# Cached keys of the samples' attention: turned by transposing DMAs on two-byte halves instead of by TensorE

## The chip, the cores and the metric

The kernel runs on one core of one Trainium2 chip. The metric is the device time of one execution in microseconds. The kernel before takes 1761.27 us (median of three runs, 1759.50 to 1762.44).

## The reference: what is computed

One layer of a decoder, for a prompt of 1024 tokens and for 8 samples with 4 new tokens each (1056 tokens in all, width 1024): a mixer (windowed attention beside a convolution), cross-attention into 256 memory tokens, and a gated feed-forward part with a short convolution. The part that the change touches is the attention of the samples in the mixer:

```python
def dilated_branch_sample(q, kc, vc, dil):
    # q: (Bd,T,H,Dh); kc,vc: (Bd, WB+T, H, Dh) = window buffer then new rows
    j = jnp.arange(KEYS_PER_BRANCH + 1)
    idx = wb + jnp.arange(T)[:, None] - dil * j[None, :]
    kg = kc[:, idxc]
    s = jnp.einsum("bthd,btjhd->bthj", q, kg) * (HEAD_DIM ** -0.5)
    ...
    o = jnp.einsum("bthj,btjhd->bthd", (p / den).astype(vc.dtype), vg)
```

It is done for the dilations 1, 4 and 16 over cached keys and values of 2048 rows of 512 numbers (8 heads of 64, float32) for each sample. Of the 2048 cached rows only 896 are ever read: the last 512, and of the older ones four rows in every sixteen (384). To score them, the head dimension must lie on the partitions, while the cache in HBM has a row per key: the keys have to be turned.

## The kernel before, in words

Everything stays in float32. The large products (input projections, output, cross-attention and feed-forward weights) run over weight units of 128 output columns: SyncE loads a unit (`weight`, line 460) into one of four ring slots (`raw`), ScalarE rounds it to a high part (line 621), VectorE makes the low part (line 1854), and TensorE does three products. The last input unit is `LAST_IN`; its end opens the attention stage.

The attention stage is one loop over steps `s`, written out by hand on each engine. A step is a pair of heads for 128 prompt queries: `STEPS` has 32 of them, 8 query tiles (`i`) times 4 pairs, and a step grows with `i`. Step `s` runs the scores of `s`, the transposes of the probabilities of `s - 2`, the product with V of `s - 3`. Between these pieces lie up to three slots a step, and slots carry the samples' work: 88 slots, 44 for each group of 4 samples (`first_slot`, `sample_slot`). The first 14 steps have three slots each, the later ones 2 or 3. In a group, slots 0 to 27 turn the key tiles (a sample has 7 tiles of 128 keys, `KTILES`), slots 1 to 28 score them, slots 29 to 34 do the softmax and turn the probabilities, slots 35, 37, 39 and 41 multiply by the values of one sample each, and slots 42 and 43 take the result out. Each engine has its own `sample(g, r)` for its share. All engines work in order, so a late key tile holds everything behind it.

The key path before: SyncE loads a window (`window`, line 472: 896 rows of one sample, keys or values, in four DMAs) into one of three buffers `cached`, in the order four key windows, four value windows, and so on (`ORDER_W`). In a key slot TensorE turns four 128 x 128 blocks of a tile into one PSUM bank (`key_turn`, line 1427, recorded under line 1237); ScalarE (line 801) or VectorE (line 2071) copies the bank to `KTS`, a third to two thirds of the tiles each (`on_scalar`); and in the next slot TensorE scores the tile (`key_scores`, line 1436, recorded under line 1240): four products for the four pairs of heads, each into its own 32 rows of a bank, against `QW`, which holds the samples' queries spread with zeros.

```python
        def key_turn(n):
            b, a = divmod(n, KTILES)
            w, c = window_of("k", b)
            take(4 + n % 2, "ktsa" if on_scalar(n) else "ktsd", n)
            pe.wait_ge(*at(f"cached{c}", (w, OLD // P - 1)))
            for k in range(AT):
                ins = turn(bank[4 + n % 2][:, k * P:(k + 1) * P], cached[c][:, a, k * P:(k + 1) * P])
            ins.then_inc(*mark("ktr", n))
```

SyncE's queue around it (lines 506 to 529): the weights up to the third output unit are issued before the last input product ends, then window 1 after it, window 2 after the convolution's tiles are free, the 19 output DMAs of V, of the convolution state and of the copied state (lines 512 to 519), then windows 3 to 15, each behind a wait for the window that its buffer held (`ktr` for keys, `spv` for values), then the fourth output weight. GpSimd does a few memsets (lines 597 to 608) and nothing else.

## Time and profile before

| | |
|---|---|
| median of 3 runs | 1761.27 us (1759.50 to 1762.44) |
| span of the profiled execution | 1761.8 us |
| attention stage | 335 to 545 us of the span |
| HBM read / written | 220.68 MB / 11.50 MB |
| mean granted clock of TensorE | 0.995 |

The page gives no time of its own for the profiled execution beside its span, from the first to the last instruction; the span is 0.5 us above the median of the runs. Line numbers are those of the kernel before. A float32 product is recorded as two instructions, a transpose as one: a row of "x8" products is four, a row of "x4" transposes is four. "128*32" before the shape is the size of the stationary part. A helper records many operations under one line: 1237 is every transpose of TensorE, 1240 every product, 458 every load of SyncE. "SPq" is SyncE issuing a DMA, and its time is that of the issue, not of the transfer. In a timeline the first column is the start in the span, the second how long the row lasts; the ends of products overlap the next row's start, so the pitch from start to start is what one takes.

### The profile page before, as it was taken

The page shows a single profiled execution, that of the slowest core. Times are in us where ns is not written, and L with a number is a line of the kernel's source. Part 1 is how long each engine was busy: PE and PEld are TensorE (multiplying, and loading weights), DVE is VectorE, ACT ScalarE, POOL GpSimd, SP SyncE. Part 2 cuts the span into 40 slices and gives each one's busy share as a digit, 9 for nine tenths or more (in the row PEclk, how much of TensorE's full clock was granted, in tenths as well). Part 3 has the DMA queues.
Part 4 walks back from the last instruction along what each step waited for, and adds up shares of the span by engine and source line. Part 5 has one row for each costly group of instructions (what it writes and reads, how often), then busy time and mean ns, then how long its engine had stood idle before and what let it go on. Part 6 is the DMA issues. An engine that isn't in the chain of part 4 may idle for free.

```text
span 1761.8 us, 30467 instructions
## 1 busy us (share of the span) xinstructions
PE 1712.2 (97%) x12158; PEld 1595.8 (91%) x12158; DVE 1127.0 (64%) x2077; ACT 876.3 (50%) x1645; POOL 2.2 (0%) x12
## 2 busy tenths in 40 slices
PE   7999999999999999999998999999999999999998
PEld 7999999756668999888778899999999999999998
DVE  5499998686675677345467667644576533676633
ACT  7322223655667676555455455534545533555433
POOL 0000000000000000000000000000000000000000
PEclk9999999999999999999999999999999999999999
DMA  8233221365315645443533334444445444444443
GB/s 247 64 119 114 84 86 37 132 225 192 127 43 154 185 144 156 149 131 108 164 120 96 118 114 140 133 136 138 133 143 155 139 140 139 132 144 147 144 136 100
DMA packets 349219, 233.74 MB, mean 133 GB/s; under 512 B 7979, under 2 KB 322465, under 8 KB 349071
## 3 DMA queue, kind: packets, MB, share of 16 engines
q1 hardware_dynamic: 344232, 222.96, 41.4%
q10 hardware_dynamic: 4847, 8.83, 1.4%
q8 instruction: 98, 1.61, 0.4%
q14 instruction: 42, 0.34, 0.1%
HBM read 220.68 MB, written 11.50 MB: 132 GB/s over the span
## 4 chain that ended last, share of the span: by engine, by line
PE 85%; DVE 7%; ACT 4%; issue 3%; SPq 1%; DMA 0%; ACTq 0%; DVEq 0%
PE bank L1240 79%; PE bank L1237 6%; ACT whi L621 1%; SPq L458 1%; DVE cv L1841 1%; DVE wlo L1854 1%; DMA raw<-in_w_mk_dram 0%; DVE Y L1841 0%; DVE Pp L1845 0%; DVE RSCF L1977 0%; DVE Pp L2130 0%; ACT wide L635 0%; DVE op_lo L1841 0%; DVE XT L2232 0%; DVE C L1981 0%
## 5 line engine op out<-in xcount | busy, mean ns | idle before, releaser
L1240 PE MATMUL bank<-op_hi,whi 128*128 128x352 f32 x1632 | 539.5, 331 | 4.9 <-DVE wlo L1854 2.6
L1854 DVE TENSOR_TENSOR wlo<-raw,whi 128x1024 fp32r<-128x1024 f32 (+1 forms) x312 | 373.8, 1200 | 246.0 <-ACT whi L621 245.7
L1240 PE MATMUL bank<-op_hi,wlo 128*128 128x352 f32 x1632 | 525.4, 322 | 0.0
L1240 PE MATMUL bank<-op_lo,whi 128*128 128x352 f32 x1632 | 524.5, 321 | 0.0
L621 ACT ACTIVATE whi<-raw 128x1024 fp32r<-128x1024 f32 (+1 forms) x312 | 325.1, 1043 | 287.7 <-PE bank L1240 94.5
L1240 PEld LDWEIGHTS bank<-op_hi,whi 128*128 128x128 f32 x1632 | 307.5, 188 | 14.6 <-issue 9.9
L1240 PEld LDWEIGHTS bank<-op_lo,whi 128*128 128x128 f32 x1632 | 308.4, 189 | 0.6
L1240 PEld LDWEIGHTS bank<-op_hi,wlo 128*128 128x128 f32 x1632 | 307.3, 188 | 0.0
L1240 PE MATMUL bank<-fhi,whi 128*128 128x352 f32 x528 | 171.2, 324 | 0.0
L1240 PE MATMUL bank<-fhi,wlo 128*128 128x352 f32 x528 | 170.7, 323 | 0.0
L1240 PE MATMUL bank<-h1hi,whi 128*128 128x352 f32 x480 | 158.0, 329 | 0.0
L1841 DVE SCALAR_TENSOR_TENSOR C<-U,cw,C 128x1024 f32<-128x1024 f32 x120 | 154.1, 1284 | 3.8
L1240 PE MATMUL bank<-h1hi,wlo 128*128 128x352 f32 x480 | 154.3, 321 | 0.0
L1240 PE MATMUL bank<-h1lo,whi 128*128 128x352 f32 x480 | 154.0, 321 | 0.0
L1240 PEld LDWEIGHTS bank<-fhi,wlo 128*128 128x128 f32 x528 | 99.8, 189 | 0.0
L1240 PEld LDWEIGHTS bank<-fhi,whi 128*128 128x128 f32 x528 | 99.4, 188 | 0.0
L1240 PEld LDWEIGHTS bank<-h1lo,whi 128*128 128x128 f32 x480 | 90.3, 188 | 0.6
L1240 PEld LDWEIGHTS bank<-h1hi,whi 128*128 128x128 f32 x480 | 90.1, 188 | 0.7
L1240 PEld LDWEIGHTS bank<-h1hi,wlo 128*128 128x128 f32 x480 | 90.1, 188 | 0.0
L1240 PE MATMUL bank<-flo_a,whi 128*128 128x352 f32 x264 | 84.9, 322 | 0.0
L1841 DVE SCALAR_TENSOR_TENSOR cv<-aext,fw,cv 128x352 f32<-128x352 f32 (+2 forms) x176 | 81.0, 491 | 3.9
L2205 DVE TENSOR_TENSOR Sy<-Sy,SQy 128x352 f32<-128x352 f32 x63 | 33.0, 524 | 70.6 <-ACT SQy L898 70.5
(287 smaller groups left out, 2299.7 us busy)
## 6 DMA issues: line engine op xcount, KB each, us to landing
raw<-in_w_up_dram SPq DMA_DIRECT2D x132, 512.0 KB, 3.7
raw<-in_w_down_dram SPq DMA_DIRECT2D x48, 512.0 KB, 3.7
raw<-in_w_out_dram SPq DMA_DIRECT2D x24, 512.0 KB, 3.8
raw<-in_w_xq_dram SPq DMA_DIRECT2D x24, 512.0 KB, 3.8
raw<-in_w_xo_dram SPq DMA_DIRECT2D x24, 512.0 KB, 3.8
raw<-in_w_in_dram SPq DMA_DIRECT2D x20, 512.0 KB, 3.8
raw<-in_w_down_dram SPq DMA_DIRECT2D x24, 384.0 KB, 3.3
cached<-in_cache_win_k_dram SPq DMA_DIRECT2D x8, 1024.0 KB, 5.9
```

The costliest lines, as they stand in the source:

```text
L458: sp.dma_start(dst, src).then_inc(*mark(name, key, 16))
L621: act.activation(whi[v % SLOTS][:, 0:nk, :], raw[v % SLOTS][:, 0:nk, :], ACT.Copy).then_inc(*mark("w_hi", v))
L1237: return pe.transpose(out, in_, ident[r:r + n, r:r + n])
L1240: return pe.matmul(out, lhsT, rhs, start=first, stop=last, skip_group_check=shared)
L1841: return dve.scalar_tensor_tensor(out=out, in0=in0, scalar=scalar, in1=in1, op0=op0, op1=op1)
L1854: dve.tensor_tensor(wlo[v % SLOTS][:, 0:nk, :], raw[v % SLOTS][:, 0:nk, :], whi[v % SLOTS][:, 0:nk, :].bitcast(F32), ALU.subtract).then_in ...
L2205: dve.tensor_tensor(Sy[:, :], Sy[:, :], SQy[:, :], ALU.add).then_inc(*mark("ysum", (name, c, m)))
```

## The change

Keys no longer pass through `cached`. SyncE issues DMAs that transpose on the way from HBM: `turn_keys(n)` turns one unit, the 896 keys of sample `n // 4` for the pair of heads `n % 4`, into `KT2`. Such a DMA works on two-byte elements, so a float32 key appears as two rows, its low and its high half. `part_keys(n)` moves even and odd rows apart with four DMAs inside SBUF into `KP`, 64 partitions each. `merge_keys` on GpSimd (pairs 0 and 1) and `sample` on ScalarE (pairs 2 and 3) copy the halves, two copies a unit, interleaved into `KM`, where they are float32 again. TensorE scores a whole sample at once (`key_scores(b)`), in the slot of its seventh key tile. `cached` has two buffers, for values alone, and the order of the old keys within a window changes from row-major to residue-major, which splits a value window's old part into six DMAs (`OLD_PIECES`). `KT2` and `KP` lie on the weight ring, so the loads of the first three output weights move behind the last merge. The diff, cut to its core:

```diff
@@ -208,11 +210,13 @@
-    cached = [mn(f"cached{i}", o, [P, KTILES, AW]) for i, o in enumerate((160064, 47104, 119808))]
+    cached = [mn(f"cached{i}", o, [P, KTILES, AW]) for i, o in enumerate((47104, 119808))]
+    KM = mn("KM", 160064, [P, AT, KEYS])
+    KT2 = [place(f"KT2_{i}", RING + o, [P, 2, KEYS], U16) for i, o in enumerate((0, 3584, 7168))]
+    KP = [place(f"KP{i}", RING + o, [P, 2, KEYS], U16) for i, o in enumerate((10752, 14336, 17920))] + [mn("KP3", 16384, [P, 2, KEYS], U16)]
     ATT = mn("ATT", 20480, [P, AT, NTOK])
...
     PT = mn("PT", 38912, [P, 2, SEQ])
-    KTS = [mn(f"KTS{i}", 16384 + 2048 * i, [P, AT, P]) for i in range(2)]
     QW = mn("QW", 61440, [P, 2, 544])
@@ -335,7 +339,15 @@
     SAMPLE = 44
-    ORDER_W = [(kind, b) for g in range(2) for kind in "kv" for b in range(4 * g, 4 * g + 4)]
+    KEY_UNITS = AT * BD
+    OLD_PIECES = []
+    for r in range(4):
+        g = 0
+        while g < OLDR:
+            a, p = divmod(r * OLDR + g, P)
+            n = min(P - p, OLDR - g)
+            OLD_PIECES.append((r, g, n, a, p))
+            g += n
     EARLY = 14
@@ -358,15 +370,12 @@
-    def window_of(kind, b):
-        n = ORDER_W.index((kind, b))
-        return n, n % len(cached)
-
-    def on_scalar(n):
-        return (n % 3 == 0) == (n < GROUP)
-
-    def product_bank(s):
-        return 3 if any(0 <= sample_slot(s + 3, pos)[1] < GROUP for pos in range(3)) else 4
+    def merged_by(k):
+        return "kmp" if k < 2 else "kma"
+
+    def batch_slot(r):
+
+        return r // KTILES if 0 <= r < GROUP and r % KTILES == KTILES - 1 else -1
@@ -469,14 +478,34 @@
-        def window(n):
-
-            kind, b = ORDER_W[n]
-            rows = A["cache_win_v" if kind == "v" else "cache_win_k"][0, b].rearrange("s h d -> s (h d)")
-            dst, name = cached[n % len(cached)], f"cached{n % len(cached)}"
-            load(dst[:, OLD // P:, :], rows[WB - NEAR:WB, :].rearrange("(a p) n -> p a n", p=P), name, (n, "near"))
-            for a in range(OLD // P):
-                load(dst[:, a, :], rows.rearrange("(g r) n -> g r n", r=16)[a * 32:(a + 1) * 32, 0:4, :], name, (n, a))
+        def window(b):
+
+            rows = A["cache_win_v"][0, b].rearrange("s h d -> s (h d)")
+            dst, name = cached[b % len(cached)], f"cached{b % len(cached)}"
+            load(dst[:, OLD // P:, :], rows[WB - NEAR:WB, :].rearrange("(a p) n -> p a n", p=P), name, (b, "near"))
+            for j, (r, g, n, a, p) in enumerate(OLD_PIECES):
+                load(dst[p:p + n, a, :], rows.rearrange("(g r) n -> g r n", r=16)[g:g + n, r, :], name, (b, j))
+
+        def turn_keys(n):
+
+            b, k = divmod(n, AT)
+            if n >= 3:
+                sp.wait_ge(*at(f"kp{(n - 3) % 2}", (n - 3, 1, 1)))
+            t, name = KT2[n % 3], f"kt{n % 2}"
+            rows = A["cache_win_k"][0, b].rearrange("s h d -> s (h d)").bitcast(U16)[:, 2 * k * P:2 * (k + 1) * P]
+            sp.dma_start_transpose(t[:, :, OLD:KEYS], rows[WB - NEAR:WB, :]).then_inc(*mark(name, (n, "near"), 16))
+            for r in range(4):
+                sp.dma_start_transpose(t[:, :, r * OLDR:(r + 1) * OLDR], rows.rearrange("(g r) n -> g r n", r=16)[0:OLDR, r, :]).then_inc(*mark(name, (n, r), 16))
+
+        def part_keys(n):
+
+            b, k = divmod(n, AT)
+            sp.wait_ge(*at(f"kt{n % 2}", (n, 3)))
+            if b:
+                sp.wait_ge(*at(merged_by(k), (n - AT, 1)))
+            for e in range(2):
+                for h in range(2):
+                    sp.dma_start(KP[k][DH * e:DH * e + DH, h, :], KT2[n % 3][h:P:2, e, :]).then_inc(*mark(f"kp{n % 2}", (n, e, h), 16))
@@ -486,7 +515,7 @@
             weight(g + 1)
-        for u in range(SLOTS, XFIRST + SLOTS - 1):
+        for u in range(SLOTS, XFIRST):
             weight(u)
@@ -497,17 +526,30 @@
                     load(stage_u[:, i, :], A["state_conv"].rearrange("a b t c -> (a b t) c")[i * 120:(i + 1) * 120, :], "states", ("u", i))
-            if u == 3 * NT:
-                window(0)
             if u == 2 * NT:
...
+        sp.wait_ge(*at("unit", LAST_IN - 3))
+        turn_keys(0)
+        turn_keys(1)
+        sp.wait_ge(*at("unit", LAST_IN - 2))
+        part_keys(0)
+        turn_keys(2)
+        sp.wait_ge(*at("unit", LAST_IN - 1))
+        part_keys(1)
+        turn_keys(3)
+        part_keys(2)
+        turn_keys(4)
         sp.wait_ge(*at("unit", LAST_IN))
-        window(1)
+        part_keys(3)
+        turn_keys(5)
+        window(0)
+        part_keys(4)
+        turn_keys(6)
         sp.wait_ge(*at("csq_used", 2 * CH - 1))
         sp.wait_ge(*at("cn", (CONV_ORDER[CH - 1], CT - 1)))
-        window(2)
+        window(1)
         sp.wait_ge(*at("ztok", ("v", AT - 1, 2)))
@@ -517,13 +559,23 @@
         sp.dma_start(O["conv_s"][0, :, 0:PAD - TD, :], A["state_conv"][0, :, TD:PAD, :]).then_inc(*mark("out", "cs", 16))
-        for n in range(len(cached), 2 * BD):
-            kind, b = ORDER_W[n - len(cached)]
-            if kind == "k":
-                sp.wait_ge(*at("ktr", b * KTILES + KTILES - 1))
-            else:
-                sp.wait_ge(*at("spv", b))
-            window(n)
+        for n in range(5, KEY_UNITS):
+            part_keys(n)
+            if n + 2 < KEY_UNITS:
+                turn_keys(n + 2)
+            if n in (5 * AT - 1, 6 * AT - 1):
+                for b in range(2 * (n // AT) - 6, 2 * (n // AT) - 4):
+                    sp.wait_ge(*at("spv", b - 2))
+                    window(b)
+        sp.wait_ge(*at("kp0", (KEY_UNITS - 2, 1, 1)))
+        sp.wait_ge(*at("kp1", (KEY_UNITS - 1, 1, 1)))
+        for k in range(AT):
+            sp.wait_ge(*at(merged_by(k), (KEY_UNITS - AT + k, 1)))
+        for u in range(SLOTS - 1):
+            weight(XFIRST + u)
+        for b in range(6, BD):
+            sp.wait_ge(*at("spv", b - 2))
+            window(b)
         for e in range(2):
@@ -603,9 +655,24 @@
         pool.memset(U[:, :, 0:PAD], 0.0).then_inc(*mark("pads", 0))
+        def merge_keys(n):
+
+            b, k = divmod(n, AT)
+            pool.wait_ge(*at(f"kp{n % 2}", (n, 1, 1)))
+            if b:
+                pool.wait_ge(*at("ssc", b - 1))
+            halves = KM[:, k, :].bitcast(U16).rearrange("p (n h) -> p h n", h=2)
+            for h in range(2):
+                pool.tensor_copy(halves[:, h, :], KP[k][:, h, :]).then_inc(*mark("kmp", (n, h)))
+
+        for k in range(2):
+            merge_keys(k)
         pool.wait_ge(*at("unit", LAST_IN))
...
         pool.memset(QO[:, :, :, :], 0.0).then_inc(*mark("qzw0", 1))
+        for b in range(1, BD):
+            for k in range(2):
+                merge_keys(AT * b + k)
@@ -793,12 +860,16 @@
-            if 0 <= r < GROUP and on_scalar(g * GROUP + r):
-                n = g * GROUP + r
-                act.wait_ge(*at("ktr", n))
-                if n >= 2:
-                    act.wait_ge(*at("ssc", n - 2))
-                act.activation(KTS[n % 2][:, :, :], bank[4 + n % 2][:, :].rearrange("p (k n) -> p k n", k=AT), ACT.Copy).then_inc(*mark("ktsa", n))
+            if 0 <= r < GROUP and r % KTILES in (1, 3):
+                b = 4 * g + r // KTILES
+                k = 2 + (r % KTILES) // 2
+                n = AT * b + k
+                act.wait_ge(*at(f"kp{n % 2}", (n, 1, 1)))
+                if b:
+                    act.wait_ge(*at("ssc", b - 1))
+                halves = KM[:, k, :].bitcast(U16).rearrange("p (n h) -> p h n", h=2)
+                for h in range(2):
+                    act.activation(halves[:, h, :], KP[k][:, h, :], ACT.Copy).then_inc(*mark("kma", (n, h)))
             if r == GROUP + 2:
@@ -1415,33 +1486,23 @@
             i, hp = STEPS[s]
-            take(product_bank(s), "att", s)
+            take(4, "att", s)
             for e in range(2):
...
                     h = 2 * hp + e
-                    ins = mm(bank[product_bank(s)][64 * e:64 * e + 64, 0:P], V[:, blk, h * DH:(h + 1) * DH], PT[:, e, blk * P:(blk + 1) * P], blk == 0, blk == i)
+                    ins = mm(bank[4][64 * e:64 * e + 64, 0:P], V[:, blk, h * DH:(h + 1) * DH], PT[:, e, blk * P:(blk + 1) * P], blk == 0, blk == i)
             ins.then_inc(*mark("pv", s))
-        def key_turn(n):
-            b, a = divmod(n, KTILES)
-            w, c = window_of("k", b)
-            take(4 + n % 2, "ktsa" if on_scalar(n) else "ktsd", n)
-            pe.wait_ge(*at(f"cached{c}", (w, OLD // P - 1)))
+        def key_scores(b):
+            g, i = divmod(b, 4)
             for k in range(AT):
-                ins = turn(bank[4 + n % 2][:, k * P:(k + 1) * P], cached[c][:, a, k * P:(k + 1) * P])
-            ins.then_inc(*mark("ktr", n))
-
-        def key_scores(n):
-            b, a = divmod(n, KTILES)
-            g, b = divmod(b, 4)
-            pe.wait_ge(*at("ktsa" if on_scalar(n) else "ktsd", n))
-            for k in range(AT):
-                col = P * (a % 4)
-                ins = mm(bank[6 + a // 4][32 * k:32 * k + 32, col:col + P], QW[:, g, P * b + 32 * k:P * b + 32 * k + 32], KTS[n % 2][:, k, :],
-                         a == 0 and b == 0, b == 3, True)
-            ins.then_inc(*mark("ssc", n))
+                pe.wait_ge(*at(merged_by(k), (AT * b + k, 1)))
+            for c0, c1, bk in ((0, 512, 6), (512, KEYS, 7)):
+                for k in range(AT):
+                    ins = mm(bank[bk][32 * k:32 * k + 32, 0:c1 - c0], QW[:, g, P * i + 32 * k:P * i + 32 * k + 32], KM[:, k, c0:c1], i == 0 and bk == 6, i == 3, True)
+            ins.then_inc(*mark("ssc", b))
@@ -1480,12 +1541,10 @@
-            if 0 <= r < GROUP:
-                key_turn(g * GROUP + r)
             if r == 1:
                 group_scores(g)
-            if 1 <= r <= GROUP:
-                key_scores(g * GROUP + r - 1)
+            if batch_slot(r) >= 0:
+                key_scores(4 * g + batch_slot(r))
             if r == GROUP + 5:
@@ -2063,14 +2122,8 @@
-            if 0 <= r < GROUP and not on_scalar(g * GROUP + r):
-                n = g * GROUP + r
-                dve.wait_ge(*at("ktr", n))
-                if n >= 2:
-                    dve.wait_ge(*at("ssc", n - 2))
-                dve.tensor_copy(KTS[n % 2][:, :, :], bank[4 + n % 2][:, :].rearrange("p (k n) -> p k n", k=AT)).then_inc(*mark("ktsd", n))
             if r == GROUP + 1:
-                dve.wait_ge(*at("ssc", (g + 1) * GROUP - 1))
+                dve.wait_ge(*at("ssc", 4 * g + 3))
                 if g:
@@ -2132,7 +2185,7 @@
             dve.wait_ge(*at("pv", s))
-            dve.tensor_copy(ATT[:, hp, i * P:(i + 1) * P], bank[product_bank(s)][:, 0:P]).then_inc(*mark("att", s))
+            dve.tensor_copy(ATT[:, hp, i * P:(i + 1) * P], bank[4][:, 0:P]).then_inc(*mark("att", s))
...
             s = SLOT["mix", c]

```

## Rows read from the trace of the kernel before

**Rows 1.** The page: busy time by engine, and the copy of ScalarE on a weight unit

```profile
PE 1712.2 (97%) x12158; PEld 1595.8 (91%) x12158; DVE 1127.0 (64%) x2077; ACT 876.3 (50%) x1645; POOL 2.2 (0%) x12
...
L621 ACT ACTIVATE whi<-raw 128x1024 fp32r<-128x1024 f32 (+1 forms) x312 | 325.1, 1043 | 287.7 <-PE bank L1240 94.5
```

**Rows 2.** Busy time by window, around the attention stage

```profile
core 0: us, PE busy (x) PEld busy (x) DVE busy (x) ACT busy (x) POOL busy (x), PEclk, DMA share, GB/s
...
300.00:335.00 35.00, 34.30 (x205) 32.59 (x203) 25.93 (x44) 23.46 (x47) 0.29 (x1) 1.00 0.11 31
335.00:545.00 210.00, 196.87 (x2315) 131.51 (x2315) 144.23 (x453) 125.12 (x284) 0.97 (x2) 0.98 0.43 151
545.00:800.00 255.00, 254.29 (x1779) 238.14 (x1778) 152.41 (x286) 157.72 (x319) 0.00 (x0) 1.00 0.51 158
```

**Rows 3.** Timeline of TensorE, 471 to 479 us: start, duration, line, tiles

```profile
471.26 0.66 PE L1237 MATMUL bank<-ident,cached 128*128 128x128 f32 x4
471.84 0.43 PE L1240 MATMUL bank<-KTS,QW 128*32 128x128 f32 x8
472.20 1.09 PE L1237 MATMUL bank<-ident,Pp 128*128 128x128 f32 x8
473.22 0.92 PE L1240 MATMUL bank<-KT,QT 64*128 64x384 f32 x4
474.07 0.66 PE L1237 MATMUL bank<-ident,cached 128*128 128x128 f32 x4
...
475.60 1.13 PE L1240 MATMUL bank<-KT,QT 64*128 64x512 f32 x4
476.66 1.53 PE L1240 MATMUL bank<-PT,V 128*64 128x128 f32 x24
478.12 0.43 PE L1240 MATMUL bank<-KTS,QW 128*32 128x128 f32 x8
```

**Rows 4.** Instructions by tile (cached, KTS, QW): count, then ns min/median/max

```profile
L1237 PE MATMUL bank<-ident,cached x224: 272/273/477, 335.6 to 474.5; 128*128 128x128 f32 x112
L1240 PE MATMUL bank<-KTS,QW x448: 272/297/423, 337.1 to 478.3; 128*32 128x128 f32 x150
L801 ACT ACTIVATE KTS<-bank x29: 572/597/599, 336.3 to 474.8; 128x512 f32<-128x512 f32 x29
L2071 DVE COPY KTS<-bank x27: 626/684/692, 339.6 to 472.8; 128x512 f32<-128x512 f32 x27
...
L607 POOL MEMSET QW<- x1: 1008/1008/1008, 334.7 to 334.7; 128x1088 f32 x1
```

**Rows 5.** Table of waits, 335 to 545 us: total, times, longest

```profile
PEld bank L1240 <- DVE KTS L2071: 6.5, 10, 2.5
PE bank L1240 <- DVE KTS L2071: 4.4, 6, 2.2
```

**Rows 6.** Timeline of SyncE's queue, 334 to 500 us

```profile
334.68 10.25 SPq L458 DMA_DIRECT2D cached<-in_cache_win_k_dram  x8
344.98 5.42 SPq L513 DMA_DIRECT2D out_dram<-V  x8
350.44 0.92 SPq L514 DMA_DIRECT2D out_dram<-V  x1
351.40 0.93 SPq L516 DMA_DIRECT2D out_dram<-cst  x1
352.38 3.14 SPq L518 DMA_DIRECT2D out_dram<-cst  x8
355.56 0.77 SPq L519 DMA_DIRECT2D out_dram<-in_state_conv_dram  x1
356.38 3.44 SPq L458 DMA_DIRECT2D cached<-in_cache_win_k_dram  x4
359.86 36.14 SPq L458 DMA_DIRECT2D cached<-in_cache_win_v_dram  x16
397.34 26.40 SPq L458 DMA_DIRECT2D cached<-in_cache_win_k_dram  x16
439.45 59.95 SPq L458 DMA_DIRECT2D cached<-in_cache_win_v_dram  x16
```

**Rows 7.** Issues under line 458: count, then ns min/median/max

```profile
L458 SPq DMA_DIRECT2D raw<-in_w_out_dram x24: 367/368/379, 293.6 to 633.1; - x24
L458 SPq DMA_DIRECT2D cached<-in_cache_win_v_dram x32: 373/602/1778, 359.9 to 498.7; - x32
L458 SPq DMA_DIRECT2D xtok<-in_x_prompt_dram x10: 378/433/606, 543.2 to 603.4; - x10
```

**Rows 8.** Timeline of TensorE: first waits for copies, fourth batch, second window product

```profile
340.38 0.66 PE L1240 MATMUL bank<-KTS,QW 128*32 128x128 f32 x8 [2.25 <-DVE KTS L2071]
344.80 1.12 PE L1237 MATMUL bank<-ident,cached 128*128 128x128 f32 x4
345.84 0.66 PE L1240 MATMUL bank<-KTS,QW 128*32 128x128 f32 x8
...
380.52 0.42 PE L1240 MATMUL bank<-KTS,QW 128*32 128x128 f32 x8
...
396.86 0.42 PE L1240 MATMUL bank<-V,PTS 32*32 32x128 f32 x8
397.21 1.13 PE L1240 MATMUL bank<-KT,QT 64*128 64x512 f32 x4
```

**Rows 9.** Busy time by window, with the granted clock (PEclk)

```profile
340.00:348.00 8.00, 7.62 (x56) 4.13 (x57) 3.64 (x13) 3.97 (x11) 0.00 (x0) 0.60 0.65 219
348.00:382.00 34.00, 32.90 (x374) 19.96 (x374) 29.25 (x94) 16.72 (x55) 0.00 (x0) 1.00 0.75 269
```

**Rows 10.** The DMA view of 360 to 375 us

```profile
DMA packets 2745, 5.27 MB, mean 352 GB/s; under 512 B 187, under 2 KB 187, under 8 KB 2742
```

**Rows 11.** The page: DMA issues, KB each, us from issue to landing

```profile
raw<-in_w_out_dram SPq DMA_DIRECT2D x24, 512.0 KB, 3.8
```

More of the change, by code:

```diff
@@ L70, in sample_bias @@
 def sample_bias():
-    old = (16 * np.arange(OLD // 4)[:, None] + np.arange(4)[None, :]).ravel()
+    old = (16 * np.arange(OLDR)[None, :] + np.arange(4)[:, None]).ravel()
     near = WB - NEAR + np.arange(NEAR)
@@ L236, in layout @@
     Yb = [mn(f"Y{i}", o, [P, NT, CW]) for i, o in enumerate((50176, 129024, 140288))]
-    STD = [place(f"STD{i}", RING + 8192 * i + 4096, [P, CW]) for i in range(CH)]
+    STD = [place("STD0", RING + 21504, [P, CW]), place("STD1", RING + 22912, [P, CW]), mn("STD2", 37376, [P, CW])]
     SQ = [mn(f"SQ{i}", 129024 + 1408 * i, [P, CW]) for i in range(4)]
@@ L1465, in window_product @@
         def window_product(b):
-            w, c = window_of("v", b)
+            c = b % len(cached)
             g = b // 4
```

6 lines of the change are left out of this document (4 added, 2 removed).

## The prediction, made before the changed kernel was built or run

> **What bounds the kernel now.** I read the page first: TensorE is busy 97% of the span, VectorE 64%, ScalarE 50%, GpSimd not at all [rows 1]. Then I cut the span around the change. In the attention stage, 335 to 545 us, TensorE is busy 196.9 of 210 us, VectorE 144.2 and ScalarE 125.1 [rows 2]; the change lies in this stage and the last 35 us before it. TensorE's list shows what the cached keys cost it: a key tile is four transposes and four small score products, 0.94 us from the start of the transposes (471.26) to the start of what follows the products (472.20) [rows 3]. There are 56 tiles, or 224 transposes [rows 4]. The table of waits adds what TensorE waits for VectorE's copies of turned tiles, 6.5 + 4.4 = 10.9 us [rows 5]. Last I read SyncE's queue, which gets most of the new work: between 335 and 545 it issues 60 loads and 19 stores, and mostly waits [rows 6].
>
> **What is removed and added.**
> - TensorE: 56 x 0.94 = 52.6 us go. Eight batches of scores come, each 512 and 384 columns in four row groups. The nearest rows are the products on KT in two row groups: 1.06 us for 512 columns (475.60 to 476.66), 0.85 us for 384 (473.22 to 474.07) [rows 3]; so 8 x 1.91 = 15.3 us. TensorE gives up 37 us, 48 with its waits for copies.
> - VectorE: 27 copies of 684 ns go, 18.5 us [rows 4].
> - ScalarE: 29 copies of 597 ns go, 17.3 us [rows 4]; 32 merging copies of 896 columns come. A 1024-column Copy takes 1.04 us [rows 1], so 0.91 each, 29 us. At 137 of 210 us this is hidden, except that ScalarE works in order and each merge waits for its DMAs, with the exponentials of the attention steps queued behind.
> - GpSimd: 32 merging copies, for which no row stands. From below: a memset of 1088 columns takes 1.01 us [rows 4], 0.83 us for 896. From above: twice VectorE's price per column, 2 x 896 x 0.684/512 = 2.4 us. Four of them stand between the scores of one batch and of the next, 3.3 to 9.6 us; that is hidden as long as the keys of a batch take longer to arrive.
> - SyncE: 32 units (four a batch), each five transposing and four parting DMAs, 288 issues; the 32 key loads go; a value window is seven loads instead of four. The three output weights are now loaded behind the last merge instead of before 335. They land in 3.8 us [rows 11] and are wanted about two steps (13 us) after the last scores, so they cost nothing; if the keys end later still, they move with them.
> - The new order of the old keys, the moved STD tiles and the fixed product bank change no instruction's size: nothing.
>
> **SyncE is where the time goes.** All this is one queue. From the end of the last input product (334.7) to the DMA that completes the last unit it holds: parting DMAs of units 3 to 31, 29 x 4 = 116; transposing DMAs of units 5 to 31, 27 x 5 = 135; value windows 0 to 5, 42; and, ahead of unit 5's parting, the 19 stores, which take 356.4 - 345.0 = 11.4 us [rows 6]. Prices of an issue: a weight 0.37 us, a window piece 0.60, a piece of x 0.43 [rows 7]; the stores of V 5.42/8 = 0.68, the small ones 3.14/8 = 0.39, single ones up to 0.93 [rows 6]. For a window piece I take 0.60, for a parting DMA (64 runs of 1792 bytes) 0.43. **A transposing DMA has no row.** The ends are 0.37 and 0.93; I take 0.68, the stores of V, near the middle and likewise on 128 partitions of SBUF with many short runs. So the last unit is issued at 334.7 + 116 x 0.43 + 135 x 0.68 + 42 x 0.60 + 11.4 = 513 us, and with 5 us for landing and merge the last scores start at **518**. Before they start at 478.1 [rows 3]. What follows them (softmax, four window products, the last steps) is unchanged and is TensorE's, so the end moves by 40 us.
>
> A second path runs through a wait: SyncE holds windows 2 and 3 until the second window product is over. Before, the fourth batch's last scores start at 380.5 and that product ends at 397.2, 16.7 us later [rows 8]. Up to the fourth batch the queue holds 20 + 32 parting, 20 + 40 transposing and 14 window DMAs; after the wait 48, 50 and 28. By this path: 334.7 + 11.4 + 16.7 + 2 x 5 + 100 x 0.43 + 42 x 0.60 + 110 t, that is 441 + 110 t with t for a transposing DMA. At 0.68 this is 516, no more than the first path; below 0.59 it rules.
>
> **Where it is seen first.** Units 5 to 7, which the second batch needs, stand behind two windows and the stores: 20 x 0.43 + 20 x 0.68 + 14 x 0.60 + 11.4 = 42 us after 334.7, complete at about 380. By then the kernel before has scored four batches [rows 8]. The 37 us that TensorE saves become waiting here. Waiting also costs clock: after 2.25 us without work TensorE's granted clock is 0.60 between 340 and 348, nearer to the 1.2 GHz level, and four transposes take 1.04 us (344.80 to 345.84) instead of 0.59 [rows 3, 8, 9]. Such losses, some 3 us each, fall mostly into time in which keys are missing anyway; I add 4 us in all. Sum against the profiled span: 1761.8 + 40 + 4 = 1805.8. That span is 0.5 us above the median of the runs, so **1805**.
>
> **The transfers themselves.** A unit has 458,752 bytes and moves twice. At the 352 GB/s of a loaded stretch [rows 10] one move takes 1.3 us and a window 5.2. Let D be the time that a unit's five transposing DMAs fill the DMA engines. The last scores then start no earlier than 334.7 + 27 D + 29 x 1.3 + 6 x 5.2 + 6 (stores of V, 2.1 MB) + 5 = 415 + 27 D. D = 1.3 gives 450, under SyncE's chain; D = 3.8 equals it. The near end for D is the plain move, the far end five DMAs of 3.8 us to landing [rows 11] with nothing overlapped, 19 us. I take a D below 3.8, since plain runs of 2 KB show no weakness at 352 GB/s, but keep the far end as a rival.
> The Trainium skill ("DMA: Bandwidth & Descriptors", Latency and other measured facts) gives 261 GB/s for a transposing DMA with a split middle dimension; by it D is an estimated 1.76 us and the transfers do not bind. No row here shows it.
>
> **Rivals.**
> 1. *SyncE's issues bind, as above:* 0.50. With 0.5 to 0.93 us for a transposing DMA the last scores start at 496 to 552, the end at 1780 to 1836 us.
> 2. *The transfers bind:* 0.25. For it: nothing in the trace is turned by DMA, and all 14.7 MB of keys would be. Against it: two or three units are in flight, so a latency alone is covered. D = 6 gives 577, which is 1860 us.
> 3. *Transposing DMAs do not overlap:* 0.08. D = 19 gives 928 for the last scores, 450 us late: 2211 us. The Trainium skill ("VectorE: DVE Perf Modes", The three transpose paths) has 1309 ns for a 128 x 128 two-byte turn by DMA; a unit has 14, an estimated 18.3 us, so by it this rival would come true. No row here shows it.
> 4. *Faster:* 0.11. Mechanism: every issue on SyncE costs the 0.37 us of a weight load. By the second path 372.8 + 252 x 0.37 = 466, 12 us earlier than before: 1750 us. TensorE could use it, since it gives up 48 us. With the other prices as I took them this decides at t = (478.1 - 441)/110 = 0.34 us, below every load's row [rows 7].
> 5. *No change:* 0.06, the band around that point, 1758 to 1765 us.
>
> **How the numbers follow.** A measurement of this kernel can tell about 0.2%, 3.5 us. Rivals 1 to 3 are slower, 0.83; the same 0.06; faster 0.11. The forecast is rival 1's number, whose own range is 1780 to 1836. The range goes down to 1750, rival 4's number, and up to 1900 (D of 7.4 us); rival 3, the top of rival 2 and the bottom of rival 4 lie outside, just under 0.2.
>
> **What would show it.** Right: TensorE idle in long stretches between 345 and 420, released by merging copies or DMAs; SyncE issuing almost without a gap from 335 to about 510; last key scores near 518; the stage 40 to 45 us longer and all before 300 as it was; a granted clock under 1 early in the stage. Rival 2: DMA share near full while SyncE waits for transposes to complete. Rival 3: the same waits at low GB/s. Rival 4: last scores before 478. Wrong in another way: merging copies on GpSimd above 4.6 us each ((16 x 0.43 + 20 x 0.68 - 1.9)/4), so that they set the pace of a batch.

## The result, and the profile after

The changed kernel takes **1930.1 us** (median of 4 runs, 1926.4 to 1932.0) against 1761.2 before: a ratio of 1.0953, 95% interval 1.0937 to 1.0969. The forecast was 1805, its range 1750 to 1900. The sign was right, the size was not: the loss is 169 us where 44 were forecast.

The page of the changed kernel: the busy rows [rows 1], the tenths of the span (TensorE's busy share and its granted clock) and the chain that ended last.

```profile
PE 1698.1 (88%) x11614; PEld 1578.0 (82%) x11614; DVE 1116.2 (58%) x2050; ACT 893.0 (46%) x1648; POOL 39.6 (2%) x44
...
PE   7999999213374899999999989999999999999999
...
PEclk9999999556786899999999999999999999999999
...
PE 73%; SPq 16%; DVE 4%; ACT 4%; issue 3%; DMA 1%; ACTq 0%; DVEq 0%
PE bank L1311 69%; SPq L498 8%; SPq L508 4%; PE bank L1308 4%; SPq L467 2%; SPq L496 2%; ACT whi L688 1%; DVE cv L1900 0%; DVE wlo L1913 0%; DMA raw<-in_w_mk_dram 0%; DVE Y L1900 0%; ACT wide L702 0%; DVE op_lo L1900 0%; DVE XT L2285 0%; DMA cached<-in_cache_win_v_dram 0%
```

All the new time is one hole. TensorE is busy 14 us less than before, yet the span is 166 us longer, and SyncE's queue (SPq) is now 16% of the chain that ended last. Three of its lines are the change's own: L498 and L496, the transposing DMAs of 96 and of 512 rows, and L508, the parting DMAs. The busy time by stage, in the windows of [rows 2]:

```profile
core 0: us, PE busy (x) PEld busy (x) DVE busy (x) ACT busy (x) POOL busy (x), PEclk, DMA share, GB/s
300.00:335.00 35.00, 32.34 (x185) 30.66 (x184) 28.43 (x44) 22.52 (x44) 5.37 (x4) 0.96 0.32 82
335.00:545.00 210.00, 69.61 (x641) 39.88 (x640) 50.86 (x185) 56.48 (x127) 19.47 (x18) 0.63 0.52 135
545.00:800.00 255.00, 202.99 (x1698) 160.43 (x1698) 140.51 (x344) 147.91 (x290) 13.88 (x12) 0.90 0.48 134
```

In the 210 us in which TensorE was busy 196.9 before it is busy 69.6, at a mean granted clock of 0.63, nearer to the 1.2 GHz level than to 2.4 GHz. No compute engine and not the DMA engines (share 0.52) are full. SyncE's list, which answers to [rows 6] and [rows 7] (start, us, line, count):

```profile
385.56 2.45 SPq L508 DMA_DIRECT2D KP<-KT  x4
388.05 1.30 SPq L496 DMA_TRANSPOSE KT<-in_cache_win_k_dram  x1
389.39 5.09 SPq L498 DMA_TRANSPOSE KT<-in_cache_win_k_dram  x4
394.58 2.45 SPq L508 DMA_DIRECT2D KP<-KT  x4
```

One unit of keys costs the queue 394.58 - 385.56 = **9.02 us**: by the rows four parting DMAs at 0.61, one turn of 512 rows at 1.30 and four turns of 96 rows at 1.27 each, 8.84 us, and 0.18 us between the rows. SyncE waits for nothing: from 335 to 640 us the table of its own waits has one row, the wait of the weight loads behind the last merges.

```profile
SPq L573 <- ACT KM L872: 4.9, 2, 3.0
```

The three lines by themselves (min, median, max ns of an issue):

```profile
L498 SPq DMA_TRANSPOSE KT<-in_cache_win_k_dram x128: 1181/1242/2385, 295.1 to 624.4; - x128
```
```profile
L496 SPq DMA_TRANSPOSE KT<-in_cache_win_k_dram x32: 1291/1305/2387, 293.7 to 619.2; - x32
```
```profile
L508 SPq DMA_DIRECT2D KP<-KT x128: 465/596/1542, 308.5 to 630.2; - x128
```

A DMA that turns 5.3 times the rows costs 5% more. TensorE's list of the first samples and of the last key scores [rows 3, 8]; the bracket is the idle time before:

```profile
350.46 3.21 PE L1311 MATMUL bank<-KM,QW 128*32 128x512 f32 x16 [2.94 <-ACT KM L872]
...
392.97 0.69 PE L1311 MATMUL bank<-PT,V 128*64 128x128 f32 x4 [35.55 <-ACT PT L912]
...
401.57 3.21 PE L1311 MATMUL bank<-KM,QW 128*32 128x512 f32 x16 [7.29 <-ACT KM L872]
...
429.38 0.69 PE L1311 MATMUL bank<-PT,V 128*64 128x128 f32 x4 [21.56 <-ACT PT L912]
...
438.60 2.98 PE L1311 MATMUL bank<-KM,QW 128*32 128x512 f32 x16 [7.48 <-ACT KM L872]
```
```profile
641.02 1.71 PE L1311 MATMUL bank<-KM,QW 128*32 128x512 f32 x16
```

The waits name "ACT PT", a copy of turned probabilities, and not the keys. The table of waits shows what held ScalarE: it works in order, and its merging copy waited for a DMA, with that copy behind it (total, times, longest).

```profile
ACT KM L872 <- DMA KP<-KT: 138.3, 9, 34.9
```

The last scores start at 641.0, 163 us after 478.1 [rows 3] (the last of their instructions at 642.2; for the runs below, "last scores" is the start of that last instruction). From there to the end the kernel takes 1287 us against 1284 before. So the whole question is why the keys are complete at 641 and not at 518.

### The profile page after: what moved, and what is told of

Read it like the earlier page. It is cut to its first block, busy times and chain, and to the rows that moved or that the text cites. A ratio compares the mean times of both kernels' runs of the same rounds, so it can differ in the third digit from the quotient of the medians.

```text
span 1928.0 us, 29635 instructions
## 1 busy us (share of the span) xinstructions
PE 1698.1 (88%) x11614; PEld 1578.0 (82%) x11614; DVE 1116.2 (58%) x2050; ACT 893.0 (46%) x1648; POOL 39.6 (2%) x44
## 4 chain that ended last, share of the span: by engine, by line
PE 73%; SPq 16%; DVE 4%; ACT 4%; issue 3%; DMA 1%; ACTq 0%; DVEq 0%
PE bank L1311 69%; SPq L498 8%; SPq L508 4%; PE bank L1308 4%; SPq L467 2%; SPq L496 2%; ACT whi L688 1%; DVE cv L1900 0%; DVE wlo L1913 0%; DMA raw<-in_w_mk_dram 0%; DVE Y L1900 0%; ACT wide L702 0%; DVE op_lo L1900 0%; DVE XT L2285 0%; DMA cached<-in_cache_win_v_dram 0%
## 5 line engine op out<-in xcount | busy, mean ns | idle before, releaser
L1900 DVE SCALAR_TENSOR_TENSOR C<-U,cw,C 128x1024 f32<-128x1024 f32 x120 | 154.1, 1284 | 3.8
L1311 PEld LDWEIGHTS bank<-PT,V 128*64 128x64 f32 x576 | 35.1, 151 | 111.9 <-issue 110.3
L1311 PE MATMUL bank<-PT,V 128*64 128x128 f32 x576 | 43.9, 302 | 89.0 <-ACT PT L912 89.0
L1904 DVE CUSTOM_DVE_ANT_0 Pp<-bank,wt 128x512 f32<-128x512 f32 (+3 forms) x64 | 35.0, 585 | 119.2 <-PE bank L1311 119.1
L872 ACT ACTIVATE KM<-KP 128x896 uint16<-128x896 uint16 x32 | 35.9, 1188 | 138.3 <-DMA KP<-KT 138.3
```

The costliest lines, as they stand in the source:

```text
L872: act.activation(halves[:, h, :], KP[k][:, h, :], ACT.Copy).then_inc(*mark("kma", (n, h)))
L1311: return pe.matmul(out, lhsT, rhs, start=first, stop=last, skip_group_check=shared)
L1900: return dve.scalar_tensor_tensor(out=out, in0=in0, scalar=scalar, in1=in1, op0=op0, op1=op1)
L1904: return dve.tensor_tensor_reduce(out=out, in0=scores, in1=bias, scale=SCALE, scalar=start, op0=ALU.add, op1=ALU.max, accum_out=acc)
```

## The experiments

Two theories stood at first. **A:** SyncE's issues set the pace, and a transposing DMA has a price of its own, 1.28 us, whatever it turns. **B:** something behind the issues does: the turning itself in the DMA engines, or the merging copies with ScalarE's order. A third question came from the forecast: what would TensorE's 37 us be worth if the keys cost nothing? Times are medians, ratios are to the kernel before in the same comparison, with a 95% interval. The cuts of code leave out the `.then_inc(...)` of each DMA.

### The price of a transposing DMA

**a_plain**

```
-  sp.dma_start_transpose(t[:, :, OLD:KEYS], rows[WB - NEAR:WB, :])
+  sp.dma_start(t[:, :, OLD:KEYS], src[:, 0:1024].rearrange("p (e n) -> p e n", e=2))
   ... and the four of the old rows likewise
```

> All 160 transposing DMAs are replaced by as many plain DMAs of the same bytes into the same tiles, from a constant input, so the samples' scores are not those of their keys; every wait, parting, merge and product stays. Theory (the price of issuing a transposing DMA on SyncE, 1.28 us each, sets the pace of a unit of keys at 9.03 us): a plain DMA costs 0.5 to 0.6 us to issue, a unit 4.95 to 5.5 us, the last scores come 95 to 110 us earlier than the changed kernel's 641.9, at 530 to 547, and the time is 1818 to 1835 us. Rival (the merging copies and ScalarE's order, not SyncE's issues, set the pace): last scores stay within 15 us of 641.9, time 1910 to 1930. If the forecast's 0.68 us was wrong only for this one instruction, the run comes near its 1805.

1831.0 us, 1.0374 (1.0354 to 1.0395); last scores at 540, 102 us earlier. The plain DMAs cost SyncE 0.59 and 0.51 us (the second is 0.47 and the gap of 0.04 behind it). 99 us come back for one kind of instruction changed, and time and last scores lie inside the theory's ranges: the merging copies do not set the pace at 9 us. The run leaves out the turning together with the price of its issue, so it can't tell these two apart; d_half, k_split and e_pool can. And 540 is well above 518, though each of these DMAs now costs less than the 0.68 of the forecast.

**d_half**

```
-  KT2 = [place(f"KT2_{i}", RING + o, [P, 2, KEYS], U16) for i, o in enumerate((0, 3584, 7168))]
+  KT2 = [place(f"KT2_{i}", RING + o, [P, 4, KEYS], U16) for i, o in enumerate((0, 7168))]
-  rows = ...bitcast(U16)[:, 2 * k * P:2 * (k + 1) * P]
+  rows = ...bitcast(U16)[:, 4 * c * P:4 * (c + 1) * P]
```

> The same computation and the same bytes, but a transposing DMA turns two units at once: 80 transposing DMAs of twice the width instead of 160; the turned tile has two buffers of double size, and the parted one three. Theory (the price is one per transposing DMA, whatever it moves): two units cost SyncE 6.44 + 4.9 = 11.3 us and a wait of about 2.7 us for the last parting of the buffer instead of 18.06, so 4 us x 14 pairs = 53 us are won: last scores near 589, time about 1875 us; 1850 if the wait is covered. Rival (the price goes by what a DMA moves, columns or bytes): a transposing DMA now takes 2.5 us to issue, and the added waits make it slower than the changed kernel, 1930 to 1970.

1901.5 us, 1.0779 (1.0757 to 1.0800); last scores at 612. The issues, in SyncE's list of this kernel:

```profile
426.96 1.94 SPq L497 DMA_TRANSPOSE KT<-in_cache_win_k_dram  x1
428.95 5.16 SPq L499 DMA_TRANSPOSE KT<-in_cache_win_k_dram  x4
434.21 5.29 SPq L509 DMA_DIRECT2D KP<-KT  x8
441.45 1.78 SPq L497 DMA_TRANSPOSE KT<-in_cache_win_k_dram  x1
```

The turns of 96 rows cost 1.29 us at twice the width, as A says. The turn of 512 rows does not stay at 1.30: it costs 1.9. So the price is fixed only up to some size between these two. A pair of units takes 14.5 us instead of 18.0, near the 14.0 expected. The last scores come 23 us later than the 589 expected. Half a microsecond a pair makes some 7 of these, and one stop of SyncE, at 501 us, most of the rest: with three parted tiles instead of four it waits there for a merging copy of ScalarE.

```profile
SPq L506 <- ACT KM L873: 14.8, 1, 14.8
```

**k_split**

```
-  sp.dma_start_transpose(t[:, :, OLD:KEYS], rows[WB - NEAR:WB, :])
+  for q in range(4):
+      sp.dma_start_transpose(t[:, :, OLD + q * P:OLD + (q + 1) * P], rows[WB - NEAR + q * P:WB - NEAR + (q + 1) * P, :])
```

> The same computation as the changed kernel, but the one DMA that turns the 512 near rows of a unit is cut into four of 128 rows: 8 transposing DMAs a unit instead of 5, the same bytes. Theory (a transposing DMA of this size costs SyncE 1.28 us whatever it turns): 3 x 1.28 x 27 = 104 us more, last scores at 745, time 2032 us. Rival 1 (the price goes by rows or bytes, so that the four cost 1.3 us together): last scores at 640 to 650, time 1928 to 1935. Rival 2 (something else sets the pace of a unit at 9.03 us and SyncE only looks full): the same.

2047.0 us, 1.1614 (1.1597 to 1.1632); last scores at 757.4, 115.2 later than the changed kernel's. In its list four turns of 128 rows take what four of 96 take:

```profile
439.41 5.11 SPq L497 DMA_TRANSPOSE KT<-in_cache_win_k_dram  x4
444.56 5.09 SPq L499 DMA_TRANSPOSE KT<-in_cache_win_k_dram  x4
449.75 2.45 SPq L509 DMA_DIRECT2D KP<-KT  x4
452.25 5.11 SPq L497 DMA_TRANSPOSE KT<-in_cache_win_k_dram  x4
```

A unit is 452.25 - 439.41 = 12.84 us; 3.82 more than 9.02, times 30 units is 115. (I had counted 27 units; the lengthening begins before 335.) The bytes are the same and the DMA engines are less busy (share 0.30 between 395 and 510, against 0.38), so this shows that the pace is set by the count of transposing DMAs.

### SyncE relieved

**e_pool**

```
-  sp.dma_start(KP[k][DH * e:DH * e + DH, h, :], KT2[n % 3][h:P:2, e, :])
+  pool.dma_start(KP[k][DH * e:DH * e + DH, h, :], KT2[n % 3][h:P:2, e, :])
```

> The same computation; the 128 parting DMAs are issued by GpSimd, not by SyncE (and the turned tiles and parted tiles have a semaphore each). Theory (SyncE's issues set the pace): a unit costs SyncE 6.44 us instead of 9.03, so the last scores come (9.03 - 6.44) x 27 = 70 us earlier, at about 572, and the time is 1855 to 1870 us, provided that GpSimd issues four parting DMAs in under 6.4 us less half a merge, that is in under 1.4 us each. Rival 1 (the transfers or the DMA engines' turning set the pace): no change, 1920 to 1935. Rival 2 (GpSimd's issue costs more than 1.4 us, and its two merges of a batch stand behind them): the pace is GpSimd's, time above 1870.

**f_both** is d_half and e_pool together.

> The whole computation: a transposing DMA turns two units at once, as in the run of that kind, and GpSimd issues the parting DMAs, as in the other. SyncE then pays 1.95 + 4 x 1.29 = 7.1 us for two units, 3.55 a unit. Theory 1 (SyncE's issues and nothing else set the pace): 27 x 3.55 = 96, windows 25, stores 11, so last scores at 475 to 490 and a time of 1768 to 1785 us. Theory 2 (with GpSimd's queue beside it the DMA engines bind: their busy share was 0.88 in the run with GpSimd's issues, at 168 GB/s): the pace is that of the transfers; the same 168 GB/s for 29.4 MB of keys and 7.3 MB of values give 218 us from about 325, last scores at 543, time 1830 us. Theory 3 (the wait of a turn for the parting of its double buffer, 4 us of landing and 2 of issue, and two buffers alone): a pair takes 7.1 + 4.1 + 4.4 + 4.0 = 19.6 us less what overlaps between the two buffers, 12 to 14 a pair: last scores 530 to 560.

e_pool takes 1880.0 us, 1.0666 (1.0641 to 1.0690), last scores at 586 and not 572; GpSimd's issues are 0.54 us each. It turns and parts every key as the changed kernel does and is 50 us faster, so it was the queue that bound there. f_both takes 1869.8 us, 1.0606 (1.0586 to 1.0626), last scores at 584, later than all three of its theories say. (The runs of these two spread by 13 us, and e_pool's profile is of its shortest run, f_both's of its longest, so 586 and 584 are not to be compared closely.) f_both is the fastest kernel here that turns all keys by DMA, and it is nowhere near 1768, where SyncE's issues alone would put it. The DMA engines are full in the first of these two windows while only 145 GB/s are moved, and 0.67 busy in the second:

```profile
400.00:450.00 50.00, 22.03 (x136) 11.07 (x136) 18.51 (x62) 21.35 (x51) 26.87 (x41) 0.64 1.02 145
450.00:500.00 50.00, 31.24 (x404) 21.36 (x408) 20.12 (x61) 16.47 (x35) 10.48 (x17) 0.76 0.67 142
```

So below SyncE's price there is a second limit, and this looked like the DMA engines.

**l_plainpool** is e_pool with a_plain's loads, **n_small** and **p_small** are l_plainpool and a_plain with an eighth of the columns in each:

```
-  sp.dma_start(t[:, :, OLD:KEYS], src[:, 0:1024]...)
+  w = NEAR if n < 3 else 64
+  sp.dma_start(t[:, :, OLD:OLD + w], src[:, 0:2 * w]...)
   ... and the four of the old rows with 12 of 96 columns
```

> As the run in which GpSimd issues the parting DMAs (1880 us, last scores 586, DMA share 0.88 between 335 and 482), but every transposing DMA is a plain one of the same bytes from a constant input, so the samples' scores are not those of their keys. SyncE then pays about 2.75 us a unit. Theory (behind the price of issuing, turning itself fills the DMA engines and binds at 6 to 7 us a unit): with plain moves the share falls under 0.75 and the last scores come at 475 to 500, time 1768 to 1795. Rival (the parting DMAs from GpSimd's queue fill the engines or bind by their own latency): share stays above 0.8, last scores at 550 or later, time above 1840.

> As the run with plain DMAs in place of the transposing ones and the parting DMAs issued by GpSimd (1832.5 us, last scores 537.5), but from the fourth unit on each of the five plain DMAs moves an eighth of its columns; count, queues, waits, parting DMAs and merges stay. Theory 1 (with the price of issuing gone, the DMA engines' time for 29.4 MB in short runs sets the pace; share 0.82 at 210 GB/s): 12.8 MB less at 210 GB/s are 61 us less, and the floor of the run with free keys, 480, is near: last scores at 480 to 500, time 1767 to 1790. Theory 2 (the chain of a sample binds: turn, part, merge, scores, on few buffers, with landing times, and the stop between the two groups of four samples): last scores stay at 525 to 540, time 1820 to 1835.

> The same cut of the columns in the run with plain DMAs and the parting DMAs on SyncE (1831 us, last scores 540). SyncE's issues are the same as in that run, 5.2 us a unit: 334.7 + 27 x 5.2 + 25 + 11 = 511 plus 8 for landing and merge if SyncE's issues alone bind: 519, time 1808. Theory 1 (the DMA engines' time made it 540): 515 to 522. Theory 2 (waits for landing and buffers did): 535 to 540, time 1825 to 1831.

l_plainpool: 1832.5 us, 1.0399 (1.0382 to 1.0417), last scores 537.5, DMA share 0.82, which fits neither of its two theories. n_small: 1827.5, 1.0373 (1.0355 to 1.0391), last scores 537.7, share 0.69. p_small: 1835.4, 1.0415 (1.0398 to 1.0433), last scores 548, share 0.53 where a_plain has 0.70; it is outside both of its theories, and later than a_plain, not earlier. Why it is 8 us later stays open. Taking away 11.6 MB (29 units of 0.459 MB, seven eighths of each) gains nothing: where nothing is turned, the second limit is **not** the engines' time for the bytes. By the trace of n_small it is the chain of a sample; no run with more buffers tests this. Part of its chain of waits:

```profile
401.49 3.47 DMA KP<-KT
404.98 0.37 SPq L498
405.39 0.47 SPq L501
405.90 0.47 SPq L501
406.42 0.49 SPq L501
406.95 3.87 DMA KT<-in_prompt_bias_dram
410.82 0.49 issue
411.31 1.35 POOL KP L653 x3
412.94 3.27 DMA KP<-KT
416.34 0.96 issue
417.30 1.17 ACT KM L877
```

A parting must land before its buffer can be turned into again, and the turn must land before it is parted: two landings of 3 to 4 us and two issues a round. The order of the steps adds a second piece. The score products of the fourth and fifth sample in the run with free keys (below), and in p_small:

```profile
381.06 3.22 PE L1304 MATMUL bank<-KM,QW 128*32 128x512 f32 x16
428.42 1.71 PE L1304 MATMUL bank<-KM,QW 128*32 128x512 f32 x16
```
```profile
428.42 3.21 PE L1314 MATMUL bank<-KM,QW 128*32 128x512 f32 x16
481.52 1.71 PE L1314 MATMUL bank<-KM,QW 128*32 128x512 f32 x16 [1.02 <-ACT KM L875]
```

Even with no keys to wait for, 47 us lie between them: the group's softmax and its four window products. Keys can run ahead only as far as the four parted tiles. In p_small SyncE goes at 5.19 us a unit almost without a gap up to the fourth sample; then the scores stop for 53 us, in which SyncE itself waits 9.3 us for a merging copy of ScalarE; then a sample takes 22 us.

What the turning adds on top, last scores at 584 to 586 instead of 538 with GpSimd's issues, was not taken apart further: the same kernel with plain loads (l_plainpool) lands its loads in 3.2 and 3.6 us, e_pool in 4.1, and e_pool's share is 0.88 at 168 GB/s where l_plainpool's is 0.82 at 210.

### What TensorE's 37 us are worth

**c_free**

```
-  act.wait_ge(*at(f"kp{n % 2}", (n, 1, 1)))
+  if n < 4:
+      act.wait_ge(*at(f"kp{n % 2}", (n, 1, 1)))
   ... the same on GpSimd; no turn_keys and part_keys for units 4 to 31
```

> Only the first sample's four units of keys are turned, parted and waited for; the other seven samples are scored on the first one's keys (their own keys are not read), with all merging copies and products kept. It shows what TensorE gets if the keys cost nothing. Theory of the prediction (TensorE gives up 37 us, 48 with its waits, and this stage is TensorE's): 1714 to 1730 us, last scores at 431 to 445. Rival (the stage is then set by something else, the chain of softmax and merging copies on ScalarE and GpSimd, or by the value windows and the clock lost in waits): last scores later than 455, time 1740 to 1765.

**1767.3 us, 1.0022 (1.0012 to 1.0032)**, just past even the rival's 1765: with keys that cost nothing the new scheme is no faster than the kernel before. Last scores at 480. The windows 335 to 482 of the kernel before, then of this run:

```profile
335.00:482.00 147.00, 138.07 (x1586) 88.00 (x1586) 103.96 (x343) 82.57 (x206) 0.97 (x2) 0.98 0.55 195
```
```profile
335.00:482.00 147.00, 116.55 (x1018) 66.42 (x1016) 92.51 (x303) 97.06 (x204) 33.58 (x30) 0.85 0.37 109
```

Busy time times granted clock is 138.07 x 0.98 = 135.3 before and 116.55 x 0.85 = 99.1 here. TensorE does give up 36 us, as forecast; all of it comes back as 21.5 us more idle time and a clock of 0.85. Some of the idle time has nothing to do with keys: `cached` has two buffers for values where there were three, so the third and fourth value window are late, and TensorE waits for them. The kernel before has no such wait, and the forecast put this term at nothing.

```profile
PE bank L1304 <- DMA cached<-in_cache_win_v_dram: 5.9, 2, 4.0
```

**g_nomerge** leaves out the merging copies of the seven later samples too, and with them their waits for the scores before; **i_pool** has all merges on GpSimd, **j_dve** all on VectorE.

```
-  for b in range(1, BD): for k in range(2): merge_keys(AT * b + k)      # GpSimd
-  for h in range(2):
+  for h in range(2 if n < 4 else 0):                                    # ScalarE
```

> As the run with free keys (only the first sample's keys are turned), and now the merging copies of the other seven samples are left out too, on GpSimd and on ScalarE; the scores still run, on the first sample's tiles. That run took 1767.3 us although TensorE's work in the stage had fallen by 36 us (its busy time times its granted clock). Theory A (the merging copies took the place: 14 us of ScalarE's copies lie on its chain of waits, and GpSimd's slow VectorE down): 1745 to 1755 us. Theory B (without the key tiles between them, TensorE waits for the softmax of the attention steps, from one engine to the next, and loses clock in those waits): 1760 to 1768, last scores of a sample still after 465.

> As the run with free keys (1767.3 us), with all four merges of a sample on GpSimd and none on ScalarE. Theory A1 (ScalarE's in-order merges stand in front of the exponentials and copies of the steps): 1752 to 1760 us. Theory A2 (GpSimd's merges slow VectorE wherever they run, and twice as many do more of it): 1770 to 1778. Theory B (the softmax chain binds whatever the merges do): 1764 to 1769; but 4 x 1.2 x 2 = 9.6 us of merges now stand between two samples' scores on one engine, which costs nothing while a sample takes over 12 us.

> As the run with free keys (1767.3 us), with all four merges of a sample on VectorE and none on GpSimd or ScalarE. Without any merges that run takes 1751.1; with all of them on GpSimd 1776.8. Theory (GpSimd's copies cost by slowing VectorE down, ScalarE's by standing before the exponentials): on VectorE a copy of 896 two-byte columns costs 0.5 to 0.95 us, 64 of them 32 to 61 us where VectorE is busy 92 of 147 us, and nothing else is slowed: 1754 to 1765. Rival (any engine that merges stands in the chain of a step, and VectorE most): 1768 to 1785.

g_nomerge: 1751.1 us, 0.9930 (0.9917 to 0.9943), last scores at 460. The merges cost 16 us, so its theory A holds. But even without them the kernel is only 12 us faster than before (0.7%), a third of the 36 that TensorE gives up. i_pool: 1776.8, 1.0084 (1.0071 to 1.0097): inside A2's range, more merges on GpSimd cost more. Part of this is not VectorE slowed down, since TensorE also waits 8.1 us for the merging copies themselves, 4.7 in c_free. j_dve: 1779.2, 1.0091 (1.0076 to 1.0106), in the rival's range and not to be told from i_pool. There the copies are only 0.66 us each, but TensorE's waits stand on VectorE:

```profile
PE bank L1288 <- DVE pmx L1881: 15.5, 11, 4.3
PE bank L1288 <- DVE KM L2112: 11.5, 4, 4.3
```

In each of the three places the merge costs 16 us or more. That it always lands in the softmax chain of an attention step is how these waits are read here; no run moves a merge within its step. The split between ScalarE and GpSimd that the change has is the best of the three.

**h_late** is c_free with GpSimd's first two merges behind the last input product.

```
+  pool.wait_ge(*at("unit", LAST_IN))
   for k in range(2): merge_keys(k)
-  pool.wait_ge(*at("unit", LAST_IN))
```

> As the run with free keys (1767.3 us), but GpSimd's first two merges run behind the end of the last input product instead of ahead of it. In the changed kernel they lie beside four VectorE multiplies that take 3.75 us instead of 1.83, and the product that needs them ends 3.6 us later than before the change. Theory (GpSimd's copies slow VectorE while both run): the four multiplies take 1.8 to 1.9 us again, the first attention scores start 2 to 3.6 us earlier than 339.0, and the time is 1763.5 to 1765.5, if the first sample's merge, now some 2 us later, does not cost it again. Rival (the multiplies are long because of something else, the parting DMAs for one): 3.7 us as before, no change in time.

1766.2 us, 1.0018 (1.0007 to 1.0029): no change in time, and the gain of 2 us or more did not come. Its reason is right nevertheless: without the copies beside them the multiplies are short again. The twelve multiplies of line 2033, in c_free and in h_late (min, median, max ns):

```profile
L2033 DVE TENSOR_TENSOR C<-C,RSCF x12: 514/520/1482, 319.2 to 330.7; 128x352 f32<-128x352 f32 x12
```
```profile
L2033 DVE TENSOR_TENSOR C<-C,RSCF x12: 516/519/527, 318.9 to 328.5; 128x352 f32<-128x352 f32 x12
```

The product ends 2.3 us earlier, and TensorE then waits 5.5 us for ScalarE's root instead of 2.9; the first sample's scores start at 349.85 against 349.70.

## Why the prediction was wrong, step by step

- **SyncE's chain binds (rival 1): right.** TensorE idle in long stretches, SyncE without a gap, clock well under 1, all before 300 as it was: each of these signs came. The queue ran to 630.8 instead of 513. (Rival 1's own ends, 1780 and 1836, leave out the 4 us of clock that the forecast adds; with them they are 1783 and 1839, and the result is outside either way.)
- **The price of a transposing DMA: the step that failed.** "I take 0.68, near the middle" of 0.37 and 0.93. It is 1.28 (6.39 us for five), above both ends. (1.28 - 0.68) x 135 = 81 of the 123 us between 518 and 641. The bounds were rows of other kinds of DMA; none of them bounded this one from above, and the text said itself that it had no row.
- **The parting DMA:** 0.61 for 0.43, (0.61 - 0.43) x 116 = 21 us. In all 102. Some 6 more are the queue's backlog: it comes to the first unit behind the last input product at 340.5, not at 334.7. From the last issue (630.8) to the scores it is 10 us for 5. Stores and windows were 3 us cheaper. The rest, some 13 us, is about 5 us between the rows and otherwise issues above their median: late in the stage a unit's four parting DMAs take 3.2 to 3.4 us, and once four turns of 96 rows take 6.52.
- **With 0.68 the forecast would still have been low.** a_plain has 0.52 us in that place and takes 1831, not under 1805. With 0.52 the forecast's own sum gives last scores at 498, and they start at 538.8. Of these 41 us 21 are the parting DMA's price again, 3 the later start, some 8 are waits of SyncE inside the stage, 4.5 the last landing, and the rest is mostly time between issues. The waits are what both paths of the forecast left out: a turn waits for the parting before it to land (4.0 us in all), and a parting for a merging copy (3.9 us), since the fifth sample's scores stand 47 us behind the fourth's in the order of the steps.
- **Transfers (rival 2, D up to 6 us): wrong as the bound, at this pace.** The DMA share was 0.38 at 103 GB/s between 395 and 510. Times 9.02 us that is an estimated 3.4 us of the DMA engines for turning and parting a unit together, in which no window moves. The share comes near full only where SyncE is relieved (e_pool, f_both).
- **No overlap (rival 3, 2211 us): wrong.** The Trainium skill ("VectorE: DVE Perf Modes", The three transpose paths) would give an estimated 18.3 us of turning for a unit; here a transposing DMA lands 2.4 us (96 rows) or 3.5 us (512 rows) after its issue, in the median, and a whole unit passes every 9.02 us. The measurement decides.
- **TensorE's work: about right, its worth: wrong.** A sample's scores take 1.64 us from start to start at full clock (641.02 to 642.66) for a forecast of 1.91, and 3.14 at half of it; 37 us of work were to go, 36 did in c_free. But the text costed ScalarE's and GpSimd's merges at nothing since each engine had time to spare. They cost 16 us with keys free. A likely reason, argued from the waits only, is that they stand between the stages of a softmax, and that the turns they replaced had filled just those waits. The late value windows (5.9 us of waits in c_free) had no term either. So rival 4's gain of 12 us did not exist at any price of issue: at a price of zero the time is 1767.
- **The merging copies:** on GpSimd 1.18 us, inside the bounds 0.83 to 2.4, and as many as forecast; on ScalarE 1.19 us for a forecast of 0.91.

What stays open: why turning costs the queue 1.28 us (no run varies anything but count and size), how much of e_pool's and f_both's 1870 to 1880 is the engines' turning and how much the chain, and whether more buffers would shorten that chain.

## What to carry to other kernels

An operation that has no row in the trace is not bounded by its nearest relatives; where the sum takes 135 of it, measure one first, and give the far side of its range real weight. In these runs a DMA has a price on the queue that issues it, per instruction and nearly whatever it moves (0.47 us for a plain one of 48 KB and of 6 KB, 1.24 and 1.30 us for turns of 96 and 512 rows): count instructions on a queue before bytes, and make few large ones. And before work is taken off the engine that is busy 97%, ask what the rest of the stage would take if the work cost nothing: a run with the work left out (here 1767 against 1763 in the same comparison) would have shown that this change could not pay.

## What the runs showed of the hardware that was not expected

- **A transposing DMA costs SyncE 1.2 to 1.3 us to issue**, at 96, 128 or 512 rows of 256 two-byte columns and at 96 rows of 512; at 512 rows of 512 columns it is 1.9 (changed kernel, k_split, d_half). A plain one with the same bytes in the same place in the queue is 0.47 to 0.59 (a_plain), and the same parting DMA is 0.60 on SyncE and 0.54 on GpSimd.
- **GpSimd's copies slow VectorE.** A VectorE multiply of 352 columns takes up to 1.48 us instead of 0.52 while a merging copy runs, and none is long once the copies are moved away (h_late). The 64 multiplies of probabilities by their denominators, of the same sizes in every kernel, have a mean of 0.52 us in the kernel before, 0.64 with half of the merges on GpSimd (c_free) and 0.75 with all of them (i_pool); it is 0.52 with the merges on VectorE itself (j_dve). The Trainium skill ("SBUF — State Buffer", SBUF: two separate sides) says that a VectorE operation with two inputs in SBUF and a GpSimd operation that reads SBUF keep each other out for a whole instruction. The multiply of 352 columns has two such inputs. By that it takes, behind a copy of 1.18 us, at most an estimated 0.52 + 1.18 = 1.70 us; the longest, 1.48, agrees.
- **Waiting costs clock as well as time.** In c_free TensorE's granted clock is 0.72 between 345 and 400 us, where the kernel before has 0.99: it was busy 43.0 of the 55 us there, 50.6 before. So the work itself gets longer: a sample's scores take 3.21 us at 350 to 381 us and 1.71 at 428.
